# Hybrid decoder step: normalized x of a tile made in the token part, x loaded once per tile, index rings of four tiles

## The chip, the cores and the metric

One core of a Trainium2 chip runs the whole program. The metric is the device time of one execution in microseconds, the median of several. Engines are TensorE (PE), VectorE (DVE), ScalarE (ACT), GpSimd (POOL) and SyncE (SP, which only issues DMAs here); they run their own instruction streams and meet at semaphores.

## What is computed

One layer of a decoder for 1024 prompt tokens and 32 sample tokens (1056 in all, D = 1024). What matters here is its last part, PEER: each token picks 16 experts in each of 8 heads, 128 experts in all, and each expert is one row u and one row v of 1024 floats.

```python
x = x + merged
x = x + peer(rmsnorm(x, g_ffn), w_query, sub_keys, expert_u, expert_v)
...
u = expert_u[eid]
act = jax.nn.gelu(jnp.einsum('cd,ced->ce', xc, u))
return jnp.einsum('ce,ced->cd', g * act, expert_v[eid])
```

`rmsnorm(x, g)` is x times the reciprocal root of the mean square of its row, times g. The outputs end with a final RMSNorm with g_final.

## The kernel before

Tokens are cut into nine tiles: eight of 128 and one of 32. The program has two blocks. The **early** block makes the input projection, attention and merge of tiles 0 to 3. The **late** block runs the token part from its start to its end, and beside it, on the other engines' free time, the router (which experts a token takes) for tiles 0 to 3, then projection, attention, samples and merge of tiles 4 to 8, then the router for these.

The **merge** makes the residual x of a tile (`x2`), its mean square, the factor (`col(k, 11)`, L1676) and x times factor (`xn`, on ScalarE, L1614). TensorE turns that for the router (L1570), VectorE scales the turned form by g_ffn (L1688), and SyncE stores it as `x_turned` (L1503). For the token part VectorE also multiplies `xn` by a g_ffn row (`g_row`, L1681, loaded at L1430 once for each merge), and SyncE stores the residual as `x_res` (L1497) and the product as `x_norm` (L1499), both in HBM.

The **token part** (class `Tokens`) walks 1056 tokens, called steps n, in blocks of 16. For a step, GpSimd gathers 128 u rows by the indices in a column of `idx` (L1786, an indirect DMA of 512 KB into one of eight slots), VectorE makes the 128 dot products with the token's x (L1936), ScalarE takes the gelu of 16 tokens, VectorE makes the weights `w_sel` (L1953), GpSimd gathers the v rows (L1795, eight slots, by fours) and TensorE sums them (L1862). A u gather waits for the dot of eight steps before; a group of v gathers waits for the sums of two groups before. x gets to all partitions by a product with a selector on TensorE (`repeat_x`, L1834), one for 32 tokens, from `xn_tile`, which SyncE loads from `x_norm` once a tile (L1801, at step 97 of the tile before, when TensorE has repeated that tile's last part). When a tile is done, VectorE adds the residual (`resid`, loaded at L1801 after the tile before has been stored, L1818), and after a root on ScalarE it scales the rows by g_final (L1960 to L1976).

All of this is woven by hand: `Pace` says how many token steps every engine has done at each step of the stage beside it, so the order on each engine is fixed in the program, and each engine works through its own order.

Of the kernel before, what the change touches and what calls it, by code (L numbers as in the profile page):

```python
# [29 lines left out]
P = 128  # L30
# [1381 lines left out]
class OutWeights:  # L1412


    def __init__(self, s, a, take):
        self.a = a
        self.rnn, self.att, self.g_row = take("w_rnn", [P, CC, D]), take("w_att", [P, CC, D]), take("g_row", [P, D])
        self.landed = [s.sem(x) for x in ("w_rnn_landed", "w_att_landed", "g_row_landed")]
        self.scaled = [s.sem(x) for x in ("rnn_scaled", "att_scaled")]
# [15 lines left out]
def merge(nc, a, c, far, ctx, door, stage, tiles, yaT, take, banks, pace_of, here=None, weights=None, after_first=None):  # L1435
# [5 lines left out]
    for k in range(NT + LAG_N):  # L1441
# [12 lines left out]
    w_rnn, w_att, g_row = held.rnn, held.att, held.g_row  # L1454
    x_in, x2 = take("x_in2", [P, 2, D]), take("x2", [P, 2, D])
    xn, xf = take("xn2", [P, D]), take("xf", [P, 2, D])
    sq, xt = take("sq", [P, 2 * CC, P]), take("xt_out", [P, KC, P])
# [9 lines left out]
    xf_ready, xt_ready, xt_stored, nothing_ready = (  # L1467
        s.sem(x) for x in ("xf_ready", "xt_ready", "xt_stored", "nothing_ready"))
    xf_stored = [s.sem(f"xf_stored{i}") for i in range(2)]
# [8 lines left out]
    def sp_part(sp):  # L1478
# [15 lines left out]
        def store(k):  # L1494
# [3 lines left out]
            sp.wait_ge(xf_ready, k + 1)  # L1498
            sp.dma_start(far.x_norm[lo:lo + rows, :], xf[0:rows, k % 2, :]).then_inc(xf_stored[k % 2], 16)  # L1499
# [38 lines left out]
        for par in range(2):  # L1538
            sp.wait_ge(x2_stored[par], 16 * len(tiles[par::2]))
            sp.wait_ge(xf_stored[par], 16 * len(tiles[par::2]))  # L1540
# [49 lines left out]
    def act_part(act):  # L1590
# [9 lines left out]
        def second(k, x):  # L1600
            rows = rows_of_tile(k)
            whole = x2[0:rows, k % 2, :]
            if x == 0:
                act.wait_ge(x2_ready, 2 * (k + 1))
                if k:
                    act.wait_ge(xf_ready, k)
# [5 lines left out]
            if x == 2:  # L1612
                act.wait_ge(rb_ready, k + 1)
                nc.scalar.activation(xn[0:rows, :], whole, ACT.Copy, scale=col(k, 11)).then_inc(xn_ready, 1)  # L1614
# [25 lines left out]
    def dve_part(dve):  # L1640
# [28 lines left out]
        def second(k, x):  # L1669
# [34 lines left out]
        dve.wait_ge(held.landed[2], 16)  # L1704
# [26 lines left out]
V_SLOTS = 8  # L1731
TOPK = 16
# [11 lines left out]
class Tokens:  # L1744


    def __init__(self, nc, c, ctx, a, far, kept):
# [3 lines left out]
        self.idx, self.gate = sb("idx", [P, NTOK], I32), sb("gate_r", [P, NTOK])  # L1751
        self.u_rows, self.v_rows = sb("u_rows", [P, U_SLOTS, D]), sb("v_rows", [P, V_SLOTS, D])
        self.xn, self.sums = sb("xn_tile", [P, D]), sb("sums", [P, D])
        self.resid, self.y_out, self.gfin = sb("resid", [P, D]), sb("y_out", [P, D]), sb("gfin", [P, D])
# [6 lines left out]
        self.xn_landed, self.resid_landed, self.gfin_landed, self.out_landed = (  # L1761
            sem(x) for x in ("xn_landed", "resid_landed", "gfin_landed", "out_landed"))
# [13 lines left out]

    def pool_to(self, pool, upto):
        nc, a = self.nc, self.a
        for b, t in self.span("pool", upto):
            if b + 1 < NB:  # L1780
# [3 lines left out]
                if n >= U_SLOTS:  # L1784
# [3 lines left out]
                    bass.IndirectOffsetOnAxis(ap=self.idx[:, n:n + 1], axis=0)).then_inc(self.u_landed[n % U_SLOTS], 16)  # L1788
            if b >= 0 and t % GROUPS == GROUPS - 1:
# [4 lines left out]
                for n in range(first, first + GROUPS):  # L1794
                    nc.gpsimd.indirect_dma_start(  # L1795
                        self.v_rows[:, n % V_SLOTS, :], None, a["expert_v"][0],
                        bass.IndirectOffsetOnAxis(ap=self.idx[:, n:n + 1], axis=0)).then_inc(landed, 16)

    def load_tile(self, sp, whole, into, landed, tile):
        lo, rows = tile * P, NS if tile == PT else P  # L1800
        sp.dma_start(into[0:rows, :], whole[lo:lo + rows, :]).then_inc(landed, 16)  # L1801

    def sp_begin(self, sp):
        self.load_tile(sp, self.far.x_norm, self.xn, self.xn_landed, 0)
# [710 lines left out]
```

## Time and profile before

| | before |
|---|---|
| median of 3 runs | 3399.2 us (3398.39 to 3399.62) |
| profiled execution, its time | 3404.3 us |
| profiled execution, its span | 3402.1 us |
| VectorE busy | 2132.1 us (63%) |
| POOL busy | 2081.0 us (61%) |
| TensorE busy | 2042.7 us (60%) |
| DMA | 1251.30 MB, mean 368 GB/s |
| of these the gathers (software queue) | 1107.43 MB |

The profiled execution is one run under the profiler; its rows give durations, the median gives the time. Busy time counts instructions that compute or, on POOL, issue a gather. The token part begins at 381 us of the span. "Landing" is the time from a DMA's issue to its completion.

### The profile page before, as it was taken

The numbers are of one execution on the slowest core, as the hardware profiler recorded it, in microseconds if no ns is written. First come the engines' busy times: TensorE is split into PE (matmuls) and PEld (weight loads), VectorE is DVE, ScalarE is ACT, GpSimd is POOL, SyncE is SP. The second block draws the span as 40 slices with busy tenths as digits, with TensorE's granted clock in tenths as the row PEclk, the third lists the DMA queues.
The fourth block names the chain that finished last, engine by engine and source line by source line (L and its number), as shares of the span: only waits on it lengthen the run. The fifth ranks groups of instructions, "written<-read, shape, count | busy, mean of one in ns | idle before, by whom it ended". The sixth has DMA issues, their size and how long they took to land.

```text
span 3402.1 us, 28445 instructions
## 1 busy us (share of the span) xinstructions
PE 2042.7 (60%) x8758; PEld 793.8 (23%) x8758; DVE 2132.1 (63%) x5404; ACT 657.4 (19%) x1245; POOL 2081.0 (61%) x2144
## 2 busy tenths in 40 slices
PE   5989366574989577554775556445544654364343
PEld 2445232231554133211321212101110210021000
DVE  5253688986666577523564968756765676578542
ACT  2361121222223144200221112101110120011001
POOL 0200277776666666634565777777777777777773
PEclk9999687786999687766887778667866777687556
DMA  3342499999999999999999999999999999999995
GB/s 112 124 168 80 163 382 393 404 383 409 406 418 418 416 401 370 385 388 356 403 414 421 410 411 417 413 420 419 419 418 420 419 418 416 420 419 410 416 419 212
DMA packets 347553, 1251.30 MB, mean 368 GB/s; under 512 B 43258, under 2 KB 49402, under 8 KB 343052
## 3 DMA queue, kind: packets, MB, share of 16 engines
q0 software_dynamic: 304128, 1107.43, 81.2%
q1 hardware_dynamic: 43276, 142.07, 11.1%
q8 instruction: 70, 1.15, 0.1%
q14 instruction: 79, 0.65, 0.0%
HBM read 1219.39 MB, written 29.96 MB: 367 GB/s over the span
## 4 chain that ended last, share of the span: by engine, by line
POOL 27%; DVE 17%; DMA 16%; issue 13%; PE 13%; ACT 3%; SPq 1%; DVEq 0%; ACTq 0%; POOLq 0%
POOL v_rows L1795 15%; POOL u_rows L1786 12%; DMA u_rows<-expert_u,idx 8%; DVE u_rows L1936 7%; DMA v_rows<-expert_v,idx 6%; PE y_acc L1862 3%; PE pair L1561 2%; PE pair L598 1%; PE pair L618 1%; PE pair L2069 1%; PE pair L1008 1%; DMA arena<-w_out 1%; PE pair L1029 1%; DVE arena L2197 1%; DVE arena L2161 1%
## 5 line engine op out<-in xcount | busy, mean ns | idle before, releaser
L1936 DVE CUSTOM_DVE_ANT_0 u_rows<-u_rows,xb 128x1024 f32<-128x1024 f32 x1056 | 1271.3, 1214 | 643.9 <-DMA u_rows<-expert_u,idx 630.4
L1786 POOL DMA_INDIRECT u_rows<-expert_u,idx x1056 | 1029.1, 974 | 681.7 <-issue 258.1
L1862 PE MATMUL y_acc<-v_rows,w_sel 128*32 128x512 f32 x4224 | 791.6, 883 | 926.2 <-DMA v_rows<-expert_v,idx 869.3
L1795 POOL DMA_INDIRECT v_rows<-expert_v,idx x1056 | 1020.9, 967 | 481.6 <-issue 310.3
L1862 PEld LDWEIGHTS y_acc<-v_rows,w_sel 128*32 128x32 f32 x4224 | 145.4, 139 | 1435.1 <-DMA v_rows<-expert_v,idx 813.5
L2069 PE MATMUL pair<-arena 128*128 128x512 f32 x576 | 290.5, 639 | 0.0
L1894 ACT ACTIVATE acts<-dots 128x16 f32<-128x16 f32 x66 | 14.3, 216 | 794.2 <-DVE dots L1936 794.0
L598 PE MATMUL pair<-arena 128*128 128x272 f32 (+1 forms) x576 | 155.1, 428 | 2.2 <-DVEq L769 1.8
L2069 PEld LDWEIGHTS pair<-arena 128*128 128x128 f32 x576 | 108.8, 204 | 175.8 <-issue 175.8
L2097 PE MATMUL pair<-arena,selx 128*128 128x64 f32 x264 | 54.4, 371 | 132.5 <-DVE arena L2219 100.0
L598 PEld LDWEIGHTS pair<-arena 128*128 128x128 f32 x576 | 111.3, 196 | 54.0 <-issue 32.2
L598 PE MATMUL bank<-arena 128*128 128x512 f32 x192 | 86.3, 609 | 0.8 <-DVEq L769 0.8
L1936 DVE DVE_READ_ACCUMULATOR2_ANT dots<- 128x1 f32 x1056 | 86.7, 82 | 0.0
L2097 PEld LDWEIGHTS pair<-arena,selx 128*128 128x128 f32 x264 | 48.8, 276 | 161.4 <-DVE arena L2219 128.1
L1016 PE MATMUL pair<-ident,arena 128*128 128x128 f32 x225 | 44.3, 331 | 59.3 <-ACT arena L1074 43.3
L1907 ACT ACTIVATE y_out<-xb 32x1024 f32<-32x1024 f32 x33 | 33.5, 1016 | 234.7 <-PE xb L1872 234.7
L1114 DVE CUSTOM_DVE_ANT_0 arena<-pair,arena 128x512 f32<-128x512 f32 (+3 forms) x64 | 38.6, 618 | 63.4 <-PE pair L1008 63.4
L1834 PE MATMUL xb<-xn_tile,selx 128*128 128x512 f32 (+1 forms) x132 | 76.1, 705 | 1.5 <-DMA xn_tile<-x_norm 1.5
L1561 PE MATMUL pair<-arena 128*128 128x512 f32 (+1 forms) x160 | 74.4, 620 | 1.5 <-DVE arena L1688 1.4
L1872 PE MATMUL xb<-sums,rep 128*32 128x512 f32 x132 | 73.7, 687 | 0.8 <-ACT sums L1899 0.8
L2119 ACT ACTIVATE gate_r<-pair 32x32 f32<-32x32 f32 (+1 forms) x144 | 26.8, 186 | 234.2 <-PE pair L2097 233.0
L1899 ACT ACTIVATE sums<-y_acc 128x512 f32<-128x512 f32 x66 | 35.8, 594 | 187.8 <-PE y_acc L1862 187.7
(294 smaller groups left out, 2413.1 us busy)
## 6 DMA issues: line engine op xcount, KB each, us to landing
u_rows<-expert_u,idx POOLq DMA_INDIRECT x1056, 10.0
v_rows<-expert_v,idx POOLq DMA_INDIRECT x1056
arena<-w_in_tiles SPq DMA_DIRECT2D x32, 512.0 KB, 6.3
arena<-w_query_by_group SPq DMA_DIRECT2D x8, 2048.0 KB, 19.6
arena<-cache_kT SPq DMA_DIRECT2D x8, 1792.0 KB, 16.6
arena<-cache_v_near SPq DMA_DIRECT2D x8, 1024.0 KB, 10.3
arena<-x_prompt SPq DMA_DIRECT2D x12, 512.0 KB, 6.9
arena<-cache_v_old SPq DMA_DIRECT2D x8, 768.0 KB, 12.4
```

The source lines that it names most:

```text
L598: last = nc.tensor.matmul(ring.bank(n)[:, 0:hi - lo], w[:, use % 3, k * P:(k + 1) * P], xnT[:, k, lo:hi], start=(k == 0), stop=(k == KC - 1))
L1016: last = nc.tensor.transpose(ring.bank(n)[:, b:b + P], held(d, h)[:, lo + b:lo + b + P], c.ident[:])
L1114: nc.vector.tensor_tensor_reduce(out=logits[:, h, lo:hi], in0=ring.bank(n)[:, 0:hi - lo], in1=bias[:, edge + lo:edge + hi], scale=1.0, sca ...
L1561: last = nc.tensor.matmul(ring.bank(n)[0:rows, :], y_of(k, g, j), w_of(g)[:, j, half * HALF:(half + 1) * HALF], start=(j == 0), stop=(j == ...
L1786: nc.gpsimd.indirect_dma_start(self.u_rows[:, n % U_SLOTS, :], None, a["expert_u"][0], bass.IndirectOffsetOnAxis(ap=self.idx[:, n:n + 1], ...
L1795: nc.gpsimd.indirect_dma_start(self.v_rows[:, n % V_SLOTS, :], None, a["expert_v"][0], bass.IndirectOffsetOnAxis(ap=self.idx[:, n:n + 1], ...
L1834: last = self.nc.tensor.matmul(self.xb[:, k % 2, half:half + HALF], self.c.selx[0:rows, block, :], self.xn[0:rows, half:half + HALF], star ...
L1862: last = nc.tensor.matmul(self.acc[g * BAND:(g + 1) * BAND, half:half + HALF], self.w_sel[:, b % 2, n, :], self.v_rows[:, (TB * b + n) % V ...
L1872: last = self.nc.tensor.matmul(self.xb[block * BAND:(block + 1) * BAND, k % 2, half:half + HALF], self.c.rep[:], self.sums[:, half:half + ...
L1936: nc.vector.tensor_tensor_reduce(out=self.u_rows[:, n % U_SLOTS, :], in0=self.u_rows[:, n % U_SLOTS, :], in1=self.xb[:, n // BAND % 2, :], ...
L2069: last = self.nc.tensor.matmul(self.qp, self.xt[:, part, :], self.w[:, g * KC + part, :], start=(part == 0), stop=(part == KC - 1))
L2097: last = self.nc.tensor.matmul(self.wide[:, block], self.selx[:, block, :], self.found[:, :, ranks], start=True, stop=True)
```

## The change

The merge keeps, for each tile, only the row factors in a small tile `factor` (128 x 9) that stays in SBUF. The store of `x_norm`, the product that makes it, `g_row` and its two loads go. The token part loads the residual x of a tile once, into one of two halves of `x_tile`, at step 65 of the tile before, after the add of the tile before that; the same rows serve the add at the end. A g_ffn row (`gffn`) is loaded once at the start of the token part. VectorE makes `xn_tile` from x, factor and g_ffn in one operation (`normal`), ahead of the first dot of all and then ahead of the dot of step 100 of each tile. `idx` and `gate` hold four tiles in place of nine, and the ScalarE copies into them wait, from tile 4 on, for the sums of the tile that stood there.

```diff
-        self.rnn, self.att, self.g_row = take("w_rnn", [P, CC, D]), take("w_att", [P, CC, D]), take("g_row", [P, D])
+        self.rnn, self.att = take("w_rnn", [P, CC, D]), take("w_att", [P, CC, D])
...
-        if i == 0:
-            sp.dma_start(self.g_row, self.a["g_ffn"].to_broadcast((P, D))).then_inc(self.landed[2], 16)
...
+    factor = lambda k: c.factor[0:rows_of_tile(k), tiles[k]:tiles[k] + 1]
...
-            sp.wait_ge(xf_ready, k + 1)
-            sp.dma_start(far.x_norm[lo:lo + rows, :], xf[0:rows, k % 2, :]).then_inc(xf_stored[k % 2], 16)
...
-                nc.vector.reciprocal(col(k, 11), col(k, 10)).then_inc(rb_ready, 1)
-            if x == 2:
-                dve.wait_ge(xn_ready, k + 1)
-                if k >= 2:
-                    dve.wait_ge(xf_stored[k % 2], 16 * (k // 2))
-                nc.vector.tensor_tensor(xf[0:rows, k % 2, :], xn[0:rows, :], g_row[0:rows, :], ALU.mult).then_inc(xf_ready, 1)
+                nc.vector.reciprocal(factor(k), col(k, 10)).then_inc(rb_ready, 1)
...
-        self.idx, self.gate = sb("idx", [P, NTOK], I32), sb("gate_r", [P, NTOK])
+        self.idx, self.gate = sb("idx", [P, HELD * P], I32), sb("gate_r", [P, HELD * P])
...
     def sp_begin(self, sp):
-        self.load_tile(sp, self.far.x_norm, self.xn, self.xn_landed, 0)
+        self.load_tile(sp, 0)
+        sp.dma_start(self.gffn[:], self.a["g_ffn"].to_broadcast((P, D))).then_inc(self.gffn_landed, 16)
         sp.dma_start(self.gfin[:], self.a["g_final"].unsqueeze(0).to_broadcast((P, D))).then_inc(self.gfin_landed, 16)
-        self.load_tile(sp, self.far.x_res, self.resid, self.resid_landed, 0)
...
-            if block == 3 and (b + 1) % BB == 0 and t == 1 and b + 1 < NB:
-                sp.wait_ge(self.xb_ready, 4 * (tile + 1))
-                self.load_tile(sp, self.far.x_norm, self.xn, self.xn_landed, tile + 1)
+            if block == 2 and (b + 1) % BB == 0 and t == 1 and b + 1 < NB and tile < PT:
+                if tile:
+                    sp.wait_ge(self.added, tile)
+                self.load_tile(sp, tile + 1)
...
-                self.load_tile(sp, self.far.x_res, self.resid, self.resid_landed, tile + 1)
...
+                if n == 0:
+                    self.normal(dve, 0)
+                if n % P == P - BAND + 4 and n // P < PT:
+                    self.normal(dve, n // P + 1)
...
+    def normal(self, dve, tile):
+        rows = NS if tile == PT else P
+        dve.wait_ge(self.x_landed, 16 * (tile + 1))
+        if tile:
+            dve.wait_ge(self.xb_ready, P // BAND * tile)
+        else:
+            dve.wait_ge(self.gffn_landed, 16)
+        self.nc.vector.scalar_tensor_tensor(out=self.xn[0:rows, :], in0=self.x_res[0:rows, tile % 2, :],
+                                            scalar=self.c.factor[0:rows, tile:tile + 1], in1=self.gffn[0:rows, :],
+                                            op0=ALU.mult, op1=ALU.mult).then_inc(self.xn_ready, 1)
...
         blocks = 1 if r == PT else 4
+        if r >= HELD and g == 0:
+            act.wait_ge(self.tok.v_free, P * (r - HELD + 1))
```

Three places show how the order moves. First VectorE, where the early block ends and the token part begins; `factor`, `x_tile` and `gffn` are the new tiles, and the two rows L1936 (L1934 in the changed kernel) are one dot. Before:

```order
L2215 SCALAR_TENSOR_TENSOR arena<-arena 128x32
L2217 RECIPROCAL arena<-arena 128x2
L1936 ISA u_rows,dots<-u_rows,xb 128x1024
L1936 ISA dots 128x1
L2219 TENSOR_TENSOR arena<-arena 128x32
L2148 MAX arena<-arena 128x8 x4
```

and now:

```order
L2225 SCALAR_TENSOR_TENSOR arena<-arena 128x32
L2227 RECIPROCAL arena<-arena 128x2
L1961 SCALAR_TENSOR_TENSOR xn_tile<-x_tile,factor,gffn 128x1024
L1934 ISA u_rows,dots<-u_rows,xb 128x1024
L1934 ISA dots 128x1
L2229 TENSOR_TENSOR arena<-arena 128x32
```

One product of 128 x 1024 stands ahead of the first dot.

Second SyncE in the late merge, the stores of its last two tiles (tile 7 and the 32-row tile); `arena` is the merge's own space. Before:

```order
L1497 DMA x_res<-arena 128x1024
L1499 DMA x_norm<-arena 128x1024
L1503 DMA x_turned<-arena 128x1024
L1497 DMA x_res<-arena 32x1024
L1499 DMA x_norm<-arena 32x1024
L1503 DMA x_turned<-arena 1024x1x32
```

and now:

```order
L1495 DMA x_res<-arena 128x1024
L1499 DMA x_turned<-arena 128x1024
L1795 DMA x_tile<-x_res 128x1024
L1495 DMA x_res<-arena 32x1024
L1499 DMA x_turned<-arena 1024x1x32
```

The store of x_norm of each tile is gone (five in all in this merge), and a load of x into `x_tile` (tile 4) has come in between.

Third SyncE in a tile of the last stage, one period and a little more. Before:

```order
L1801 DMA xn_tile<-x_norm 128x1024
L2026 DMA arena<-x_turned 128x1024
L1818 DMA out_y_prompt<-y_out 128x1024
L1801 DMA resid<-x_res 128x1024
L2026 DMA arena<-x_turned 128x1024
L1801 DMA xn_tile<-x_norm 128x1024
```

and now:

```order
L2034 DMA arena<-x_turned 128x1024
L1813 DMA out_y_prompt<-y_out 128x1024
L2034 DMA arena<-x_turned 128x1024
L1795 DMA x_tile<-x_res 128x1024
L1813 DMA out_y_prompt<-y_out 128x1024
```

Of two loads a tile for the token part (`xn_tile` and `resid`) one is left, and it stands behind the load of the next turned tile, not behind the store of y.

## Rows read from the trace of the kernel before

**Rows 1.** Windows by stage: busy us of each engine, PEclk, DMA share, GB/s.

```profile
430.00:800.00 370.00, 240.85 (x1016) 99.03 (x1016) 338.40 (x1055) 77.81 (x193) 267.58 (x274) 0.80 1.00 393
800.00:1200.00 400.00, 301.45 (x1305) 155.84 (x1306) 242.67 (x498) 107.33 (x164) 262.45 (x269) 0.84 1.02 414
1200.00:1410.00 210.00, 153.42 (x957) 73.88 (x957) 149.89 (x361) 91.35 (x139) 142.66 (x146) 0.83 0.98 382
1410.00:1650.00 240.00, 110.82 (x658) 32.87 (x662) 73.33 (x152) 26.50 (x38) 96.16 (x102) 0.64 1.01 384
1650.00:1880.00 230.00, 165.01 (x652) 63.88 (x648) 135.19 (x277) 37.49 (x62) 141.28 (x146) 0.85 1.02 413
1900.00:3330.00 1430.00, 714.73 (x2964) 197.40 (x2964) 955.57 (x2336) 171.31 (x376) 1083.03 (x1121) 0.72 1.02 417
...
1480.00:1490.00 10.00, 5.28 (x33) 2.40 (x25) 5.08 (x13) 3.35 (x4) 2.50 (x3) 0.50 1.02 431
```

**Rows 2.** L1786, landings in windows 800:1200, 1410:1650, 1650:1880, 1900:2000, 3250:3330.

```profile
DMA to landing us min/median/max: 5.1/14.0/18.0
...
DMA to landing us min/median/max: 6.8/22.5/46.7
...
DMA to landing us min/median/max: 8.4/12.1/35.1
...
DMA to landing us min/median/max: 5.8/5.9/8.3
...
DMA to landing us min/median/max: 11.1/11.3/11.6
```

**Rows 3.** Timeline, last stage: gathers and VectorE products beside them.

```profile
2009.15 0.95 POOL L1786 DMA_INDIRECT u_rows<-expert_u,idx  x1 [0.30 <-issue]
2010.40 1.72 POOL L1786 DMA_INDIRECT u_rows<-expert_u,idx  x1 [0.30 <-issue]
...
3008.14 1.51 POOL L1786 DMA_INDIRECT u_rows<-expert_u,idx  x1 [0.30 <-issue]
...
2010.08 1.23 DVE L1960 TENSOR_TENSOR y_out<-y_out,resid 128x1024 f32<-128x1024 f32 x1 [1.35 <-ACT y_out L1907]
...
3007.55 1.28 DVE L1976 SCALAR_TENSOR_TENSOR y_out<-y_out,y_stat,gfin 128x1024 f32<-128x1024 f32 x1
```

**Rows 4.** Waits of POOL in 1900:3330: us in total, times, longest.

```profile
POOL u_rows L1786 <- DVE dots L1936: 29.6, 88, 1.4
```

**Rows 5.** The chain that ended last, 3300 to the end.

```profile
3333.16 12.90 DMA v_rows<-expert_v,idx
```

**Rows 6.** Timeline, end of the early merge: VectorE, ScalarE, SyncE.

```profile
355.39 0.16 DVE L1676 RECIPROCAL region<-region 128x1 f32<-128x1 f32 x1 [1.68 <-ACT region L1611]
358.82 1.22 DVE L1681 TENSOR_TENSOR region<-region 128x1024 f32<-128x1024 f32 x1 [0.59 <-ACT region L1614]
359.96 0.74 DVE L2171 MAX8 arena<-arena 128x8 f32<-128x256 f32 x2
...
369.31 0.68 DVE L1688 TENSOR_TENSOR region<-bank,g_ffn_T 128x512 f32<-128x512 f32 x1
...
368.15 0.60 ACT L2137 ACTIVATE arena<-pair 128x512 f32<-128x512 f32 x1 [1.31 <-PE pair L2086]
...
370.08 0.32 SPq L1503 DMA_DIRECT2D x_turned<-region  x1
```

**Rows 7.** Timeline, start of the token part, and a DMA issue row.

```profile
384.68 3.78 PE L1834 MATMUL xb<-xn_tile,selx 128*128 128x512 f32 x4 [1.50 <-DMA xn_tile<-x_norm]
...
390.77 1.22 DVE L1936 CUSTOM_DVE_ANT_0 u_rows<-u_rows,xb 128x1024 f32<-128x1024 f32 x1 [9.41 <-DMA u_rows<-expert_u,idx]
...
gfin<-g_final SPq DMA_DIRECT2D x1, 512.0 KB, 5.2
```

**Rows 8.** Timeline around the late merge's weights: SyncE and VectorE.

```profile
1598.55 6.30 SPq L1430 DMA_DIRECT2D arena<-g_ffn  x1
...
1642.15 2.74 DVE L1702 TENSOR_SCALAR arena<-arena,par 128x1024 f32<-128x1024 f32 x4 [20.61 <-DMA arena<-w_out]
```

More of the change, by code:

```diff
@@ L1416, in __init__ @@
         self.a = a
[L1417 to L1418 removed]
+        self.rnn, self.att = take("w_rnn", [P, CC, D]), take("w_att", [P, CC, D])
+        self.landed = [s.sem(x) for x in ("w_rnn_landed", "w_att_landed")]
         self.scaled = [s.sem(x) for x in ("rnn_scaled", "att_scaled")]
@@ L1453, in merge @@
     held = weights or OutWeights(s, a, take)
-    w_rnn, w_att, g_row = held.rnn, held.att, held.g_row
+    w_rnn, w_att = held.rnn, held.att
     x_in, x2 = take("x_in2", [P, 2, D]), take("x2", [P, 2, D])
-    xn, xf = take("xn2", [P, D]), take("xf", [P, 2, D])
-    sq, xt = take("sq", [P, 2 * CC, P]), take("xt_out", [P, KC, P])
+    xn = take("xn2", [P, D])
+    xt, sq = take("xt_out", [P, KC, P]), take("sq", [P, 2 * CC, P])
     yr = None if here else take("y_rnn", [P, 3, CC, P])
@@ L1466, in merge @@
         s.sem(x) for x in ("sqb_done", "msb_ready", "rtb_done", "rb_ready", "xn_ready"))
-    xf_ready, xt_ready, xt_stored, nothing_ready = (
-        s.sem(x) for x in ("xf_ready", "xt_ready", "xt_stored", "nothing_ready"))
-    xf_stored = [s.sem(f"xf_stored{i}") for i in range(2)]
+    xt_ready, xt_stored, nothing_ready = (
+        s.sem(x) for x in ("xt_ready", "xt_stored", "nothing_ready"))
     yr_of = lambda k: here.y[:, :, k * P:(k + 1) * P] if here else yr[:, k % 3, :, 0:rows_of_tile(k)]
@@ L1613, in second @@
                 act.wait_ge(rb_ready, k + 1)
-                nc.scalar.activation(xn[0:rows, :], whole, ACT.Copy, scale=col(k, 11)).then_inc(xn_ready, 1)
+                nc.scalar.activation(xn[0:rows, :], whole, ACT.Copy, scale=factor(k)).then_inc(xn_ready, 1)
         pace.act(act, -1)
@@ L1731 @@
 V_SLOTS = 8
+HELD = 4
 TOPK = 16
@@ L1775, in span, with column @@
         return [(x // TB - 1, x % TB) for x in steps]
+    def column(self, held, n, width=1):
+        at = n % (HELD * P)
+        return held[:, at:at + width]
     def pool_to(self, pool, upto):
@@ L1796, in pool_to, with load_tile @@
                         self.v_rows[:, n % V_SLOTS, :], None, a["expert_v"][0],
-                        bass.IndirectOffsetOnAxis(ap=self.idx[:, n:n + 1], axis=0)).then_inc(landed, 16)
-    def load_tile(self, sp, whole, into, landed, tile):
+                        bass.IndirectOffsetOnAxis(ap=self.column(self.idx, n), axis=0)).then_inc(landed, 16)
+    def load_tile(self, sp, tile):
         lo, rows = tile * P, NS if tile == PT else P
-        sp.dma_start(into[0:rows, :], whole[lo:lo + rows, :]).then_inc(landed, 16)
+        sp.dma_start(self.x_res[0:rows, tile % 2, :], self.far.x_res[lo:lo + rows, :]).then_inc(self.x_landed, 16)
     def sp_begin(self, sp):
-        self.load_tile(sp, self.far.x_norm, self.xn, self.xn_landed, 0)
+        self.load_tile(sp, 0)
+        sp.dma_start(self.gffn[:], self.a["g_ffn"].to_broadcast((P, D))).then_inc(self.gffn_landed, 16)
         sp.dma_start(self.gfin[:], self.a["g_final"].unsqueeze(0).to_broadcast((P, D))).then_inc(self.gfin_landed, 16)
-        self.load_tile(sp, self.far.x_res, self.resid, self.resid_landed, 0)
     def sp_to(self, sp, upto):
@@ L1828, in repeat_x @@
         rows = NS if tile == PT else P
-        pe.wait_ge(self.xn_landed, 16 * (tile + 1))
+        pe.wait_ge(self.xn_ready, tile + 1)
         if k >= 2:
@@ L1949, in dve_to @@
                 dve.wait_ge(self.gelu_done, ub + 1)
-                nc.vector.tensor_tensor(self.share[:], self.acts[:], self.gate[:, TB * ub:TB * (ub + 1)],
+                nc.vector.tensor_tensor(self.share[:], self.acts[:], self.column(self.gate, TB * ub, TB),
                                         ALU.mult).then_inc(self.share_ready, 1)
@@ L1958, in add @@
         dve.wait_ge(self.y_kept, min(P // BAND * (tile + 1), NTOK // BAND))
-        dve.wait_ge(self.resid_landed, 16 * (tile + 1))
-        self.nc.vector.tensor_tensor(self.y_out[0:rows, :], self.y_out[0:rows, :], self.resid[0:rows, :],
+        self.nc.vector.tensor_tensor(self.y_out[0:rows, :], self.y_out[0:rows, :], self.x_res[0:rows, tile % 2, :],
                                      ALU.add).then_inc(self.added, 1)
@@ L2113, in act_spread @@
         blocks = 1 if r == PT else 4
+        if r >= HELD and g == 0:
+            act.wait_ge(self.tok.v_free, P * (r - HELD + 1))
         for x, held in enumerate((self.tok.gate, self.tok.idx)):
-            here = held[:, P * r:P * r + BAND * blocks].rearrange("p (c i) -> p c i", i=BAND)
+            here = self.tok.column(held, P * r, BAND * blocks).rearrange("p (c i) -> p c i", i=BAND)
             for k in range(4):
@@ L2292, in __init__ @@
         self.x_res = dram("x_res", (NTOK, D))
-        self.x_norm = dram("x_norm", (NTOK, D))
         self.x_turned = dram("x_turned", (PT + 1, P, KC, P))
@@ L2323, in program @@
         c.selx, c.rep = s.sb("selx", [P, 4, P]), s.sb("rep", [P, BAND])
+        c.factor = s.sb("factor", [P, PT + 1])
         c.par, c.coef = s.sb("par", [P, CC, N_ROWS]), s.sb("coef", [P, 2, CC])
@@ L2350, in program @@
             merging = merge(nc, a, c, far, held, Doorway(left, 2), "merge_early", early, yaT,
-                            Arena(region, 2 * CC * D + D + 2 * CC * WAVE * P).take, banks, along, here, weights,
+                            Arena(region, 2 * CC * D + 2 * CC * WAVE * P).take, banks, along, here, weights,
                             lambda sp: router.load_tokens(sp, 0))
```

14 lines of the change are left out of this document (6 added, 8 removed).

## The prediction, on record before the changed kernel ran

> **What bounds the kernel now.** I read the windows by stage first [rows 1]. From 430 us on, the mean share of the DMA engines is 0.98 to 1.02 in every stage, so the 16 engines always have something to move. That doesn't yet say that bytes set the time, so I looked at who is waited for: how long a gather of u rows takes to land, and what GpSimd (POOL), which issues the gathers, waits for.
>
> The landing time tells the queue in front of the DMA engines [rows 2]. Just after 1900 us it is 5.9 us: that is a gather with next to no queue. In 800 to 1200 it is 14.0 us, in 1410 to 1650 22.5, in 1650 to 1880 12.1: there a queue stands, slots come back late, POOL issues fewer gathers, and bytes are time. In 1900 to 3330 it creeps up from 5.9 to 11.3 us.
>
> The long last stage (1900 to 3330, 1430 us) is paced by POOL itself. Two gathers follow each other every 1.25 us (2009.15, 2010.40) [rows 3], of which 0.95 is the instruction and 0.30 the gap. 1121 gathers [rows 1] x 1.25 = 1401 us; POOL's busy time is 1083.0, which is 18 above 1121 x 0.95, from gathers that took longer; together 1419 of the 1430 us. Its real waits there are nearly nothing: 88 waits for dots of 0.34 us each, of which 0.30 is the usual gap [rows 4]. So here fewer bytes don't make the pace faster. They only keep the queue from growing, which is paid at the end: the last v gather issued in pace (3333.16) takes 12.9 us to land and the end of the program hangs on it [rows 5].
>
> In 430 to 800 VectorE is 338.4 of 370 us busy [rows 1]: it sets the pace with the router's work. In 1200 to 1410 no queue stands (DMA at 382 GB/s) and VectorE, TensorE and POOL alternate.
>
> **The change part by part.** A tile of 512 KB is 0.524 MB, 1.27 us at 413 GB/s [rows 1]; one gather moves as much.
>
> (a) Early merge. Four products L1681 and four stores of x_norm go. Around 254 to 335 us TensorE is the bound and they are hidden. The last one isn't: VectorE has its factor at 355.39, then sits in order before L1681, which waits for the scaled x until 358.82 and takes 1.22; the router work behind it then runs to the last L1688 at 369.31, and SyncE's last store at 370.08 follows at once [rows 6]. Without it that work starts some 4 us earlier, but the next L1688 needs TensorE's transposes (which need the same scaled x), and ScalarE's last copy ends at 368.75. I take -2.7 us for the store; bounds 0 and -4.4 (the whole stretch from 355.55 to 359.96).
>
> (b) Start of the token part. Before, x_norm lands and TensorE repeats it at 384.68 for 3.78 us, ready 2.2 us before the first gather is used at 390.77 [rows 7]. Now the g_ffn row goes out in the place of g_final (5.2 us to landing; issued at some 381.4, so 386.6), then the product on VectorE (1.28, by L1976, the same operation and shape [rows 3]), then 3.78 on TensorE: 391.7, and the first dot moves to 391.8. +1.0; bounds 0 and +2.5.
>
> (c) 430 to 800. One product (for tile 1) on the busy VectorE: +1.3. The x_norm load that goes is replaced by the residual load that now comes here. Bounds 0 and +1.3.
>
> (d) 800 to 1200, bytes bound. Two tile loads fewer (two residual loads and one x_norm load before, one x load now): -1.05 MB at 414 GB/s = -2.5; bounds 0 and -2.5. Its product lies in waits for u rows.
>
> (e) 1200 to 1410. No queue, bytes free. The product for tile 3: half of 1.28, +0.6; bounds 0 and +1.3.
>
> (f) 1410 to 1650. The second load of the g_ffn row goes. SyncE spent 6.30 us issuing it, ahead of the eight w_out pieces, and VectorE stood 20.6 us until they had landed at 1642.15 [rows 8], with POOL waiting behind its dots. But the queue is full, so the last piece comes by bytes: 0.52 MB, -1.3. Bounds 0 and -6.3 (the whole issue time).
>
> (g) 1650 to 1880, bytes bound. Five x_norm stores (2.23 MB), a residual load and an x_norm load go, one x load comes (SyncE's rows of the late merge in the section on the change): -2.75 MB at 413 GB/s = -6.7; bounds -3 (if half lies beside the stage's own chain of TensorE and VectorE) and -6.7. The five L1681 products there are in VectorE's waits, worth nothing.
>
> (h) 1900 to 3330. Four products, one a tile, at the hundredth dot. VectorE has room (955.6 of 1430 us). But an operation of VectorE with two inputs in SBUF makes the gather beside it longer: beside L1960 (2010.08) the gather took 1.72, beside L1976 (3007.55) 1.51, against 0.95 [rows 3]. All four L1976 of the stage did so, and L1960 in three of five. I take 0.55 each: +2.2, straight on POOL's pace; bounds 0 and +3.8 (0.95 each). The Trainium skill (SBUF — State Buffer, Who interferes with whom) says that VectorE with two SBUF inputs contends with reads of GpSimd and not with its writes, and infers that descriptor generation needs only the write side; that would make this term 0. The rows contradict the inference for these indexed gathers, and the rows decide.
>
> (i) The end. After 1900 us 2.1 MB less are moved (four residual loads and four x_norm loads before, four x loads now): 5.0 us of queue, and (h) gives the engines 2.2 us more to catch up. So the 11.3 us of landing fall to the floor of 5.9: -5.4, paid once, at the gather of 3333.16. Bounds 0 and -7 (12.9 to 5.9).
>
> The ring of four tiles for idx and gate costs no instruction. ScalarE's new wait asks for the v rows of a tile four back, while the router is one tile ahead of the tokens: never late. The load now waits for the add of the tile before, done some 40 steps earlier; SyncE is held less than by the old wait for xb.
>
> Sum: -2.7 +1.0 +1.3 -2.5 +0.6 -1.3 -6.7 +2.2 -5.4 = -13.5 us. The profiled execution took 3404.3 us, 0.15% above the median of 3399.2; the difference is taken from the median: 3385.7.
>
> **Rivals.**
> - All bytes pay at once: the 6.5 MB that leave after 430 us at 416 GB/s = 15.6, with (a), and 5.0 of SyncE's issue time in (f), less 5.1 for the products in (b), (c), (e) and (h): -18.2, 3381.0. For it: the share of 1.0 throughout. Against it: a floor of 5.9 in parts of the last stage.
> - The queue at the end isn't the DMA engines' own limit, and doesn't shrink with the bytes: without (i) -8.1, 3391.1. For it: in 1900 to 3330 the mean is 417 GB/s while a window with many cache loads has 431 [rows 1], so there may be room. The Trainium skill (DMA: Bandwidth & Descriptors, Where 436 GB/s comes from) has a ceiling of 436 GB/s; by it 419 GB/s of gathers would leave 4% free and no queue would build. The trace has one that grows from 5.9 to 11.3 us, which speaks against.
> - The stages' own chains set the time in 800 to 1880, and bytes only stood beside them: (d), (f), (g) are 0: -3.0, 3396.2. For it: in the late merge TensorE and VectorE are busy 165 and 135 of 230 us and wait for each other. Against it: landing 12 to 22 us, and POOL issues 146 gathers in 230 us there [rows 1], one per 1.58 us, where it could do 1.25.
> - Slower: the products stand ahead of the dots. Each holds the next dot back by 1.28, the slot comes back that much later, and POOL, which has eight u slots, stops. Nine times 1.28 = 11.5, with 3.8 of longer gathers, (a) and (i), and no byte that pays: +7.2, 3406.4. It decides from the point where a slot's round (landing, dot, reissue) exceeds 8 x 2.5 = 20 us; there landing is 11.3 to 12.9 [rows 2, 5], so some 5 us are to spare. Against it, then, in the last stage at least.
>
> **How the numbers follow.** Chances: the forecast 0.42, all bytes 0.20, no gain at the end 0.16, chains 0.16, slower 0.06. 0.2% is 6.8 us, about what can be told from no change. Faster by more: the forecast and all bytes nearly whole (0.60) and most of the third (0.14): 0.74. Same: 0.20. Slower: 0.06. The range goes from beyond "all bytes" with (a) and (f) at their bounds, 3377, to "chains", 3397.
>
> **What would show it.** (a) the last SyncE store of the early merge about 3 us earlier; (b) first dot about 1 us later after the barrier; (d), (g) stages 800 to 1200 and 1650 to 1880 shorter by 2.5 and 6.7 at the same GB/s; (h) four gathers beside the new product at 1.3 to 1.8, and the time for the 1121 gathers 2 us longer, not shorter; (i) landing near 6 us at 3300, and the last v gather in pace landing in 6 to 8 us. I am wrong if the landing at the end stays above 10, if the last stage gets shorter by the bytes, or if POOL's waits for dots grow.

## The result, and the profile after

The changed kernel is slower: 3439.8 us median (3436.3 to 3442.2, 4 runs) against 3399.4 us for the kernel before (3398.4 to 3399.7, 4 runs), taken beside it. The ratio is 1.0116, 95% interval 1.0104 to 1.0129. The prediction was 3385.7 us, with 0.06 on slower. The profiled execution took 3436.26 us (span 3434.4).

The windows by stage of the changed kernel, with the columns of [rows 1]:

```profile
430.00:800.00 370.00, 244.28 (x1016) 99.77 (x1016) 337.04 (x1049) 75.89 (x192) 267.12 (x272) 0.78 1.00 391
800.00:1200.00 400.00, 295.69 (x1288) 152.81 (x1280) 236.78 (x485) 101.15 (x155) 259.83 (x265) 0.85 1.02 405
1200.00:1410.00 210.00, 152.31 (x915) 72.04 (x917) 148.87 (x361) 93.28 (x141) 141.89 (x144) 0.81 0.99 379
1410.00:1650.00 240.00, 111.28 (x721) 33.66 (x713) 75.72 (x153) 29.06 (x42) 99.80 (x106) 0.67 1.02 378
1650.00:1880.00 230.00, 160.09 (x642) 61.72 (x643) 132.10 (x271) 38.31 (x63) 138.28 (x144) 0.82 1.03 411
1900.00:3330.00 1430.00, 707.29 (x2920) 200.09 (x2924) 946.59 (x2319) 166.80 (x370) 1065.65 (x1099) 0.69 1.02 407
```

Against [rows 1], the DMA share is the same 1.02 in the long stages, but the engines move less in it: 405 instead of 414 GB/s in 800 to 1200, and 407 instead of 417 after 1900, 2.4% less. In the last stage POOL issues 1099 gathers instead of 1121. In 430 to 800, where VectorE sets the pace, the rate is nearly as before (391, 393).

How long a u gather takes to land in the changed kernel, in 1900 to 2000 and in 3250 to 3330 (compare [rows 2]):

```profile
DMA to landing us min/median/max: 5.9/6.7/7.8
...
DMA to landing us min/median/max: 12.7/12.8/13.0
```

What POOL waited for in 1900 to 3330, apart from issuing (compare [rows 4]; us in total, times, longest). The first two rows are the changed kernel's, the third is the kernel before:

```profile
POOL v_rows L1789 <- PE y_acc L1856: 36.2, 47, 2.0
POOL u_rows L1780 <- DVE dots L1934: 22.1, 66, 1.1
...
POOL v_rows L1795 <- PE y_acc L1862: 2.8, 3, 1.1
```

The landing at the end is 12.8 us, not 6: the queue is longer than before. POOL, which waited 2.8 us for v slots before, waits 36.2 us for them, 47 times. POOL no longer paces the stage alone: slots come back late because the DMA engines move less. The chain that ended last in the changed kernel shows the same at its end; its v gather in pace takes 12.66 us where [rows 5] has 12.90:

```profile
3367.56 12.66 DMA v_rows<-expert_v,idx
3380.26 3.69 PE y_acc L1856 x16
...
3387.95 5.76 DMA v_rows<-expert_v,idx
```

The bytes did leave: the page has 1242.12 MB for the changed kernel and 1251.30 MB for the one before, with the same 1107.43 MB of gathers. So the change did what it says, and the bytes that stay became dearer.

The start went as the prediction had it. SyncE's last store of the early merge and the first rows of the token part (compare [rows 6, 7]):

```profile
366.65 0.32 SPq L1499 DMA_DIRECT2D x_turned<-region  x1
377.37 0.33 SPq L1795 DMA_DIRECT2D x_tile<-x_res  x1
...
383.62 1.28 DVE L1961 SCALAR_TENSOR_TENSOR xn_tile<-x_tile,factor,gffn 128x1024 f32<-128x1024 f32 x1 [5.93 <-DMA gffn<-g_ffn]
...
388.78 1.22 DVE L1934 CUSTOM_DVE_ANT_0 u_rows<-u_rows,xb 128x1024 f32<-128x1024 f32 x1 [3.87 <-PE xb L1828]
```

The store stands at 366.65 instead of 370.08 and the first dot at 388.78 instead of 390.77.

**Where the time appears.** A gather has the same number in every version, so its start is a clock for the program. The durations below are the differences of POOL's start times of the u gathers 0, 128, 256, 384, 512 and 1054 in the timelines of the profiled executions, and from there to the end of the span (us):

| kernel | start of 0 | to 128 | to 256 | to 384 | to 512 | to 1054 | to the end | span |
|---|---|---|---|---|---|---|---|---|
| before | 385.1 | 338.2 | 367.5 | 390.2 | 466.3 | 1379.6 | 75.2 | 3402.1 |
| changed | 381.4 | 342.5 | 372.3 | 394.4 | 462.7 | 1407.3 | 73.7 | 3434.4 |
| e1 | 383.6 | 340.3 | 367.1 | 390.7 | 465.1 | 1381.7 | 69.0 | 3397.4 |
| e2 | 385.9 | 338.3 | 373.7 | 395.3 | 469.8 | 1415.1 | 77.0 | 3455.1 |
| e3 | 381.4 | 340.0 | 371.5 | 393.8 | 463.2 | 1407.3 | 75.0 | 3432.1 |
| e4 | 383.4 | 342.4 | 367.9 | 390.5 | 455.1 | 1388.7 | 68.2 | 3396.1 |
| e6 | 381.2 | 339.8 | 368.5 | 389.7 | 464.4 | 1377.3 | 73.8 | 3394.7 |
| e7 | 386.9 | 338.3 | 367.1 | 391.9 | 458.8 | 1376.6 | 73.2 | 3392.9 |
| e8 | 383.6 | 339.7 | 364.6 | 390.6 | 453.8 | 1375.9 | 72.3 | 3380.4 |
| e9 | 381.2 | 342.3 | 368.9 | 390.4 | 459.7 | 1378.2 | 72.5 | 3393.2 |
| e10 | 382.7 | 340.1 | 371.0 | 394.6 | 461.1 | 1409.1 | 74.5 | 3433.1 |

Each row is one execution, and executions of one version spread by some 11 us (e1 from 3388.3 to 3399.4, e4 from 3387.0 to 3398.0), so a difference of two or three us in one column says little. The e numbers are the experiments below.

The spans differ by 32.3 us (the profiled execution of the kernel before was a long one). Of this, 27.7 us lie between gather 512 and 1054, and 4 to 5 us in each of the three columns to 128, 256 and 384; the column to 512, which holds the late merge, is shorter. In the last stage the loss comes evenly: u gathers 768 to 1024 take 667.4 us instead of 653.1, 2.2% more. That is a price per gather, not an event. The column to 128 doesn't belong to it: e4 and e9 have the same 342 us there without the loss, and e2 has the loss with 338.3.

### The profile page after: what moved, and what is told of

Its sections match the earlier page's. It is cut to its first block, busy times and chain, and to the rows that moved or that the text cites. A ratio compares the mean times of both kernels' runs of the same rounds, so it can differ in the third digit from the quotient of the medians.

```text
span 3434.4 us, 28416 instructions
## 1 busy us (share of the span) xinstructions
PE 2036.5 (59%) x8758; PEld 791.9 (23%) x8758; DVE 2133.1 (62%) x5404; ACT 657.2 (19%) x1245; POOL 2088.2 (61%) x2144
## 2 busy tenths in 40 slices
DMA packets 345009, 1242.12 MB, mean 362 GB/s; under 512 B 42954, under 2 KB 49098, under 8 KB 340508
## 3 DMA queue, kind: packets, MB, share of 16 engines
q0 software_dynamic: 304128, 1107.43, 81.9%
## 4 chain that ended last, share of the span: by engine, by line
DMA 26%; POOL 17%; PE 16%; DVE 16%; issue 10%; ACT 2%; another core or an unknown queue 0%; DVEq 0%; ACTq 0%; SPq 0%; POOLq 0%
DMA v_rows<-expert_v,idx 13%; DMA u_rows<-expert_u,idx 11%; POOL v_rows L1789 11%; DVE u_rows L1934 7%; POOL u_rows L1780 6%; PE y_acc L1856 6%; PE pair L1556 2%; PE pair L598 2%; PE pair L2077 1%; PE pair L618 1%; DMA arena<-cache_kT 1%; PE pair L1008 1%; PE pair L1029 1%; DMA arena<-cache_v_old 1%; DVE arena L2207 1%
## 5 line engine op out<-in xcount | busy, mean ns | idle before, releaser
L1934 DVE CUSTOM_DVE_ANT_0 u_rows<-u_rows,xb 128x1024 f32<-128x1024 f32 x1056 | 1273.3, 1216 | 670.5 <-DMA u_rows<-expert_u,idx 646.8
L1789 POOL DMA_INDIRECT v_rows<-expert_v,idx x1056 | 1033.9, 979 | 511.5 <-issue 293.3
L1934 DVE DVE_READ_ACCUMULATOR2_ANT dots<- 128x1 f32 x1056 | 87.5, 83 | 0.0
L1866 PE MATMUL xb<-sums,rep 128*32 128x512 f32 x132 | 73.7, 687 | 0.8 <-ACT sums L1893 0.8
```

Source lines behind the costliest of these rows:

```text
L1789: nc.gpsimd.indirect_dma_start(self.v_rows[:, n % V_SLOTS, :], None, a["expert_v"][0], bass.IndirectOffsetOnAxis(ap=self.column(self.idx, ...
L1866: last = self.nc.tensor.matmul(self.xb[block * BAND:(block + 1) * BAND, k % 2, half:half + HALF], self.c.rep[:], self.sums[:, half:half + ...
L1934: nc.vector.tensor_tensor_reduce(out=self.u_rows[:, n % U_SLOTS, :], in0=self.u_rows[:, n % U_SLOTS, :], in1=self.xb[:, n // BAND % 2, :], ...
```

## The experiments

**The theories.** What costs per byte and wasn't in the working: where the bytes go. The change adds `factor` (36 bytes a partition, which takes 64) ahead of the arena in SBUF, and everything allocated behind it moves. The addresses per partition in the two compiled programs, with the remainder by 256:

```
            before            changed
arena       20736   (0)       20800   (64)
u_rows     134912   (0)      130624   (64)
v_rows     167680   (0)      163392   (64)
```

Theory P (placement): each of a gather's rows of 4096 bytes now starts between two multiples of 256, and the DMA engines take some 2.4% longer for it. Rival R1: x_norm is gone from HBM, so the tensors behind it have other addresses there. Rival R2: the change's own work (products, waits, the load's place) slows the gathers.

**e1, factor padded.** The changed kernel with everything that stands behind `factor` moved back to multiples of 256. `region` belongs to the early block and starts where `idx` starts later, so its length moves nothing:

```diff
-REGION = 25700
+REGION = 25600
...
-        c.factor = s.sb("factor", [P, PT + 1])
+        c.factor = s.sb("factor", [P, 64])
```

> The changed kernel with its new tile factor made 256 bytes a partition instead of 36 (and the arena's region shortened by 100 words), so that everything allocated behind it in SBUF, arena, u_rows and v_rows among it, starts again on a multiple of 256 bytes a partition as in the kernel before; no instruction is added, taken away or moved. Placement theory (the gathers and loads land 64 bytes off and the DMA engines take some 2.4% longer for them): about 3386 us, landing after 1900 us near 6 us and 416 to 420 GB/s. Rival, the change's own work or its HBM addresses: 3440 us, as the changed kernel, 405 to 410 GB/s in the last stage.

3396.8 us median (12 runs) against 3400.2 (23 runs), ratio 0.9984 (0.9975 to 0.9993). A tile of 64 floats in the place of 9 takes the whole loss of 40 us away, with the same work and the same tensors in HBM, so R1 and R2 fall as its cause. Of the gain of 13.5 us that was predicted, 3 us are there by the medians and 5 by the ratio.

**e2, before shifted.** The other way round, on the kernel before:

```diff
+        pad = s.sb("pad", [P, 16])
         arena = s.sb("arena", [P, ARENA])
```

> The kernel before with an unused tile of 64 bytes a partition allocated ahead of the arena, so that arena, u_rows and v_rows start 64 bytes behind a multiple of 256; nothing else is changed. Placement theory: slower by what the placement costs, 3399 + 54 = 3453 us, with some 407 GB/s in the last stage. Rivals (the change's own products, loads and waits, or HBM addresses): 3399 us, 417 GB/s.

3456.2 us (4 runs), ratio 1.0162 (1.0148 to 1.0177): 56 us for an unused tile of 64 bytes. The last stage reads:

```profile
1900.00:3330.00 1430.00, 709.95 (x2923) 197.68 (x2921) 943.70 (x2336) 166.79 (x370) 1057.97 (x1093) 0.70 1.02 407
```

The same 407 GB/s as in the changed kernel, with none of its edits. The loss is larger here than in the changed kernel, 56 us against 40; the section on the prediction comes back to this.

**e3, x_norm kept.** The changed kernel with the tensor still declared in HBM:

```diff
         self.x_res = dram("x_res", (NTOK, D))
+        self.x_norm = dram("x_norm", (NTOK, D))
```

> The changed kernel with x_norm still declared in HBM though nothing writes or reads it, so that every tensor in HBM has the address that it had in the kernel before. HBM address theory: 3386 to 3399 us. SBUF placement theory and the theory that the change's own work is to blame: 3440 us both.

3442.3 us (4 runs), ratio 1.0127 (1.0112 to 1.0141), and 407 GB/s after 1900. The HBM addresses have no part in it.

**e4, rows aligned.** Only the gathers' targets and the tiles behind them on multiples of 256; arena, region, idx and gate stay 64 bytes off:

```diff
+        self.pad = sb("pad", [P, 48])
         self.u_rows, self.v_rows = sb("u_rows", [P, U_SLOTS, D]), sb("v_rows", [P, V_SLOTS, D])
```

> The changed kernel with 192 unused bytes a partition ahead of u_rows: u_rows, v_rows and what is allocated behind them start on multiples of 256 bytes again, while arena, region, idx and gate stay 64 bytes off. Placement theory with the gathers' targets as the cause: 3386 to 3395 us. If the placement of arena and region (merge loads, stores) were the cause, or no placement at all: 3440 us.

3395.0 us (10 runs), ratio 0.9978 (0.9968 to 0.9988). The targets of the gathers are what counts: the tiles behind them, which move along, take part in under 1% of the bytes, and the placement of arena and region, which take and give most of the other 11%, shows nothing here. The landing at 3250 to 3330 is now near the floor, as the prediction's term (i) had it:

```profile
DMA to landing us min/median/max: 6.1/6.2/6.8
```

**e5, the gathers alone.** Eight slots, indexes made by an iota, nothing beside them, one execution; the target moved by an offset in floats (`LOADS` has pairs of target and source):

```python
GATHERS = [0, 16, 0, 32, 8, 1, 48]
LOADS = [(0, 0), (16, 0), (32, 0), (0, 16), (16, 16)]
...
        def slot(off, i):
            return rows[:, off + i * D:off + (i + 1) * D]
```

> None of the reference's computation, its outputs are left unwritten: 120 gathers of 128 rows of 4 KB from expert_u for each of seven places of the target in SBUF (0, 64, 0, 128, 32, 4 and 192 bytes behind a multiple of 256 a partition), with eight slots and nothing else beside them, then 120 plain loads of the same size on the queues of SyncE and ScalarE for each of five pairs (target and source 0 or 64 bytes off, target 128 off). Theory that pieces are cut at 256 bytes of the target: 0 keeps POOL's pace of 1.25 us a gather (419 GB/s); 4, 32, 64, 128 and 192 all drop alike, to some 1.29 us (407 GB/s). Theory of a 64-byte or 128-byte unit: 64 or 128 would run as 0 does. Theory that no placement matters when nothing else runs: all seven alike at 1.25 us.

Windows of the steady part of each phase, in the order of the two lists (columns: window, length, POOL busy, PEclk, DMA share, GB/s):

```profile
30.00:130.00 100.00, 75.28 (x82) 1.00 1.03 420
190.00:290.00 100.00, 74.24 (x80) 1.00 1.03 410
350.00:450.00 100.00, 75.28 (x82) 1.00 1.03 420
510.00:610.00 100.00, 75.40 (x81) 1.00 1.03 410
670.00:770.00 100.00, 74.89 (x80) 1.00 1.03 410
830.00:930.00 100.00, 74.91 (x81) 1.00 1.03 409
1000.00:1080.00 80.00, 60.35 (x65) 1.00 1.03 410
1140.00:1240.00 100.00, 0.00 (x0) 1.00 1.03 420
1280.00:1380.00 100.00, 0.00 (x0) 1.00 1.03 410
1430.00:1530.00 100.00, 0.00 (x0) 1.00 1.03 410
1580.00:1680.00 100.00, 0.00 (x0) 1.00 1.03 419
1740.00:1840.00 100.00, 0.00 (x0) 1.00 1.03 410
```

420 GB/s with the target on a multiple of 256, 409 to 410 when it is 4, 32, 64, 128 or 192 bytes off; plain loads the same (420 and 410). Two things about the size of the effect: it does not grow with the offset, and the source may lie 64 bytes off for 419. The plain loads keep eight in flight, and each takes 10.0 us to land (10.2 with the target off), eight times the 1.25 us that 512 KB take at 420 GB/s. So 420 and 410 are ceilings here.

The gathers reach them too. Alone, POOL issues one in 1.24 us, which asks for 422 GB/s. Their landing, aligned (30 to 130) and then 64 bytes off (190 to 290):

```profile
DMA to landing us min/median/max: 6.4/6.7/6.9
...
DMA to landing us min/median/max: 7.1/8.7/10.0
```

In the kernel a gather takes 1.25 us when nothing lengthens it (419 GB/s), and with the longer ones and the other traffic the last stage moves 413 to 417 GB/s on the mean with aligned targets (413 in e4, 415 in e1, 417 in the kernel before). That lies between the two ceilings. This is why the change was felt: before, the ceiling stood just above what the stage asks for, after it below.

The Trainium skill (DMA: Bandwidth & Descriptors, How a descriptor splits into AXI transactions) has reads cut at multiples of 256 bytes, with a further transaction for one that starts between two. The loads with a source 64 bytes off show next to nothing of it (419 against 420 GB/s); the side on which this case finds the price, the written one, the page doesn't speak of. That 17 pieces in the place of 16 are the cause would fit the unit of 256, but no run counted pieces.

**e6 and e9, half of the gathers.** dots (64 bytes) between u_rows and v_rows of e4, so that v_rows is off; and the mirror, the changed kernel's u_rows off and v_rows put right:

```diff
+        self.u_rows = sb("u_rows", [P, U_SLOTS, D])
+        self.dots = sb("dots", [P, TB])
+        self.v_rows = sb("v_rows", [P, V_SLOTS, D])
```

```diff
+        self.u_rows = sb("u_rows", [P, U_SLOTS, D])
+        self.pad = sb("pad", [P, 48])
+        self.v_rows = sb("v_rows", [P, V_SLOTS, D])
```

> As the changed kernel with its gather targets on multiples of 256 (3395 us), but dots (64 bytes a partition) now stands between u_rows and v_rows, so that v_rows and the tiles behind it lie 64 bytes off while u_rows doesn't: half of the gathers land misaligned. If each misaligned gather costs its own share: 3395 + 23 = 3418 us. If the cost is only what exceeds POOL's pace of 1.25 us a gather (aligned ones have slack that the others can use): well under half, 3397 to 3405 us.

> The mirror of the run with v_rows off: in the changed kernel u_rows stays 64 bytes off, and 192 unused bytes stand behind it so that v_rows and the tiles after it start on multiples of 256. Theory of a ceiling (half of the gathers at 410 and half at 420 GB/s give 415, just under the 416 to 419 that POOL's pace and the other traffic ask for, so the queue grows and the pace holds): as there, 3396 us, with 11 us of landing at 3300. Rival, that only the u gathers' targets matter and the v gathers' don't: 3440 us.

e6: 3396.0 us (10 runs), ratio 0.9986 (0.9977 to 0.9996). e9: 3395.3 us (10 runs), ratio 0.9978 (0.9960 to 0.9996). Either half alone costs nothing that can be told from e1 and e4, both together cost some 44 us. The window of the last stage in e6, and the landing of its u gathers in 3250 to 3330:

```profile
1900.00:3330.00 1430.00, 711.55 (x2968) 196.38 (x2972) 959.25 (x2336) 170.53 (x371) 1084.11 (x1121) 0.70 1.02 416
```

```profile
DMA to landing us min/median/max: 11.0/11.0/11.6
```

The same two views of e9:

```profile
1900.00:3330.00 1430.00, 716.97 (x2972) 198.04 (x2972) 959.96 (x2333) 169.65 (x367) 1084.22 (x1121) 0.70 1.02 415
```

```profile
DMA to landing us min/median/max: 8.8/9.7/10.4
```

Both windows have 1121 gathers, so POOL's pace is as before. This is the ceiling at work: half at 410 and half at 420 make 415 (an estimate from e5), the stage asks for about as much, so the queue grows (landing 11.0 and 9.7 instead of 6.2) but the eight slots of each kind take it up. Of the two theories for e6, "each pays its share" (3418) fell; the other, 3397 to 3405, was still a little too dear. For e9 the ceiling gave 3396 and a landing of 11 us, against 3395.3 and 9.7.

**e10, 128 bytes off.** e4 with a pad of 64 bytes instead of 192:

```diff
-        self.pad = sb("pad", [P, 48])
+        self.pad = sb("pad", [P, 16])
```

> The changed kernel with 64 unused bytes a partition ahead of u_rows, so that u_rows, v_rows and what is behind them lie 128 bytes off a multiple of 256 instead of 64. Theory that only multiples of 256 count, as the gathers alone showed (410 GB/s at 128 as at 64): 3440 us, as the changed kernel. If 128 is enough beside the kernel's other traffic: 3395 us.

3438.7 us (4 runs), ratio 1.0105 (1.0062 to 1.0148), 407 GB/s after 1900. As in e5, 128 is no better than 64.

**e7, the bytes alone.** With the placement put right the change is worth 5 to 8 us by the ratios (3 to 5 by the medians) and not 13.5, so its terms were priced one kind at a time. The kernel before with x_norm's late stores and its tile loads cut to one row each:

```diff
-            sp.dma_start(far.x_norm[lo:lo + rows, :], xf[0:rows, k % 2, :]).then_inc(xf_stored[k % 2], 16)
+            sp.dma_start(far.x_norm[lo:lo + (rows if tiles[k] < WAVE else 1), :], xf[0:(rows if tiles[k] < WAVE else 1), k % 2, :]).then_inc(xf_stored[k % 2], 16)
...
+        if into is self.xn and tile:
+            rows = 1
```

> The kernel before with the traffic of x_norm cut to one row a transfer: the late merge stores one row of each tile instead of 128 and the token part loads one row of each tile from the second on, so the normalized x of those tokens is that of the first tile; no instruction is added or taken away. This prices the bytes of the change alone: 2.0 MB of stores in 1650 to 1880, and 3.7 MB of loads, half of them after 1900 us. By the prediction's terms (bytes where a queue stands, and a shorter landing at the end): -13 us, 3387. If bytes only stood beside the stages' own chains and the landing at the end has other causes: -2 to 0, 3398.

3395.4 us (12 runs), ratio 0.9984 (0.9973 to 0.9994): -5.4 us, -2 to -9. The 13 us of the prediction's byte terms lie outside the interval. By the table, one execution each, the columns to 256 and 384 give nothing together (759.0 against 757.7), the late merge gives 7.5, the last two columns 5.0 (1449.8 against 1454.8). The queue at the end did not vanish; the first v gather of the final chain still took:

```profile
3325.95 10.57 DMA v_rows<-expert_v,idx
```

**e8, the products cut.** e4 with the new product on 8 of 1024 columns for the tiles from the second on:

```diff
+        w = 8 if tile else D
-        self.nc.vector.scalar_tensor_tensor(out=self.xn[0:rows, :], in0=self.x_res[0:rows, tile % 2, :],
+        self.nc.vector.scalar_tensor_tensor(out=self.xn[0:rows, 0:w], in0=self.x_res[0:rows, tile % 2, 0:w],
```

> The changed kernel with aligned gather targets (3395 us), in which the product that normalizes x works on 8 columns instead of 1024 for the tiles from the second on (so those tokens use mostly the first tile's normalized x); waits, loads and order stay. It prices the products: by the prediction's terms 1.3 in 430 to 800, 0.6 in 1200 to 1410 and 2.2 of longer gathers after 1900 us, so 4 us faster, 3391. If VectorE's order costs more (the product ahead of a dot holds the slots back): 9 to 11 us faster, 3385. If nothing hangs on them: 3395.

3388.7 us (12 runs, from 3382.0 to 3398.3), ratio 0.9974 (0.9963 to 0.9985), against 0.9978 for e4: 1.4 us by the ratios, 6.3 by the medians, whose intervals overlap. The predicted 4 us lie between. The 9 to 11 us that the products would cost if they held the slots back don't show, but where the price lies between 0 and 6 us can't be told from this run.

The products' effect on the gathers can be read directly. The first of the four in the last stage, in the timelines of e1 and of e8:

```profile
2206.30 1.28 DVE L1961 SCALAR_TENSOR_TENSOR xn_tile<-x_tile,factor,gffn 128x1024 f32<-128x1024 f32 x1
2206.85 1.55 POOL L1780 DMA_INDIRECT u_rows<-expert_u,idx  x1 [0.30 <-issue]
...
2190.46 0.22 DVE L1963 SCALAR_TENSOR_TENSOR xn_tile<-x_tile,factor,gffn 128x8 f32<-128x8 f32 x1
2189.68 0.94 POOL L1781 DMA_INDIRECT u_rows<-expert_u,idx  x1 [0.30 <-DVE dots L1935]
```

The gathers beside the four products took 1.55, 1.79, 1.46 and 1.26 us in e1 instead of 0.95: 2.3 us together, against 2.2 in term (h). In e4 it was 2.8 us. In e8, with the product cut to 8 columns, all four took 0.94, so it is the product that lengthens them. In the changed kernel itself the products met the gathers otherwise (1.13, 1.12, 1.14 and 1.01) and cost 0.6 us.

## Why the prediction was wrong

**The step that failed** is the one that took the rate of the DMA engines as given. Every byte term was priced "at 413 GB/s" or 414 from [rows 1], with the remark that stages 800 to 1200 and 1650 to 1880 would be shorter "at the same GB/s"; the new tile `factor` has no term in the sum, which puts it at nothing without a reason, and of the ring it says that it "costs no instruction". True of instructions, but a tile also has a place. Both edits move the targets of all 2112 gathers: the shorter rings by 4352 bytes, which is 17 times 256 and harmless, the factor by 64, which is not. The runs put 43 to 45 us in its place: 3439.8 against 3396.8 and 3395.0 for the same kernel with aligned targets (e1, e4), and 56 us on the kernel before (e2). An estimate from e5: 1107.43 MB of gathers take 64 us longer at 410 than at 420 GB/s; where POOL or VectorE paces, a part of it is hidden. The rivals had no such case, and the one that ended slower (products ahead of dots) is not what happened: e1 has the same products and is not slower. Of the signs that the prediction named for being wrong, the first came (a landing above 10 us at the end, 12.8); POOL's waits for dots, the sign of that rival, fell from 29.6 to 22.1 us.

**How little room there was.** The reading that POOL paces the last stage at 1.25 us was right and is what makes this case sharp: the stage moved 417 GB/s on the mean, 0.7% below the ceiling of 420. The prediction saw the queue grow from 5.9 to 11.3 us and wondered whether there was room up to 431 GB/s. e5 shows none above 420 for such rows. The 436 GB/s that it takes from the Trainium skill (DMA: Bandwidth & Descriptors, Where 436 GB/s comes from) no run here reached. A resource at 99% should have been asked what would make it 2% dearer, not only what relieves it.

**What the same bytes are worth on either side of the ceiling.** e2 and the changed kernel have the same placement (64 bytes off) and the same 407 GB/s, and the changed one is the faster by 16 us (3439.8 against 3456.2; ratios 1.0116 and 1.0162). The 6.5 MB that by the prediction's count leave after 430 us are 16 us at 407 GB/s, an estimate. So where the ceiling lies below what the stages ask for, the rival "all bytes pay" (18.2 us) fits, though no run took these bytes away by themselves with the targets off; with aligned targets the same change is worth 5 to 8 us.

**Its other steps**, read on the four versions in which the placement costs no time (e1, e4, e6, e9; table above, against the kernel before, one execution each, so within two or three us):

| step | predicted | measured, e1 / e4 / e6 / e9 |
|---|---|---|
| (a)+(b) start of gather 0 | -1.7 | -1.5 / -1.7 / -3.9 / -3.9 |
| (c) to 128 | +1.3 | +2.1 / +4.2 / +1.6 / +4.1 |
| (d)+(e) to 384 | -1.9 | +0.1 / +0.7 / +0.5 / +1.6 |
| (f)+(g) to 512 | -8.0 | -1.2 / -11.2 / -1.9 / -6.6 |
| (h)+(i) to the end | -3.2 | -4.1 / +2.1 / -3.7 / -4.1 |
| sum, by the spans | -13.5 | -4.7 / -6.0 / -7.4 / -8.9 |

- (a), (b): right within some 2 us; the start moved as told.
- (c): the column is 1.6 to 4.2 us longer, but that is not shown to be the product's price: e8, without the product of tile 1, has 1.5 there as well (339.7 against 338.2). By gather 128 the start's gain is gone in most versions; what takes it back stays open.
- (d): wrong. Landings of 14 us in 800 to 1200 were taken as bytes being time; 1.05 MB less gave nothing in four versions, nor did e7's part of it. The stage moves 414 GB/s where e5 has a ceiling of 420, so it seems that a queue stands there at times and bytes still are not what it waits for all along; with the ceiling at 410 the same two columns lost 9.0 us. The "chains" rival was right for this stage, in the sense that fewer bytes bring nothing; which engine holds it in their place was not tested.
- (f), (g): the mean of -5.2 is nearer to the 8.0 than to nothing, yet it spreads over 10 us between versions that differ in placement alone, and e4, which gains 11.2, gives 9.1 back in the column to 1054. From gather 384 to the end the four are 5.3, 9.1, 5.6 and 10.7 us shorter, against 11.2 in the prediction. e7 gives 7.5 for its bytes in one execution. What in the late merge decides between -1 and -11 was not settled.
- (h): right in mechanism and size for e1 and e4, as the rows above show; in the changed kernel the size was 0.6. The inference of the Trainium skill (SBUF — State Buffer, Who interferes with whom) that descriptor generation is free of VectorE's reads does not hold for these gathers, by the 1.26 to 1.99 us of e1 and e4 against the 0.94 of e8.
- (i): right where all targets are aligned. The landing fell to 6.2 us (e4), and the tail from 75.2 to 69.0 (e1) and 68.2 us (e4), -6.2 and -7.0 against -5.4. In e6 and e9, with a ceiling of 415, the queue stays (11.0 and 9.7 us) and the tail gains 1.4 and 2.7, but the pace is kept.

With aligned targets the change is 0.9984 (0.9975 to 0.9993, e1) and 0.9978 (0.9968 to 0.9988, e4), 5 to 8 us faster than the kernel before. The two can't be told apart, and the forecast of 13.5 was too large for both, by (c), (d) and the unsettled (f), (g). The range of 3377 to 3397 holds both medians, near its upper end; what it left out is the placement.

## What to carry to other kernels

An edit that adds, drops or resizes a tile moves every tile allocated behind it: compare the addresses of the DMA targets before and after, and keep the targets of the heavy streams on multiples of 256 bytes a partition (seen here for rows of 4 KB). Here, with the demand one or two per cent below the DMA ceiling, transfers 2.4% dearer cost 2.2% in the last stage, and half of that only a longer queue and no time, so look at how far the demand stands below the ceiling before pricing either direction. When a change costs a constant share per gather over a thousand gathers, look at what all of them share, not at the edited instructions.

## What the runs showed of the hardware that was not expected

- Rows of 4 KB from HBM into SBUF: 420 GB/s with the target on a multiple of 256 bytes a partition, 409 to 410 at 4, 32, 64, 128 and 192 bytes off, for indexed gathers and plain loads alike (e5, e10). The profile's DMA share is 1.02 to 1.03 in both, so it doesn't tell the two apart; GB/s does.
- A source that starts 64 bytes behind a row's start in HBM: 419 GB/s, next to free (e5).
- With half of the gathers off, in either half, 415 to 416 GB/s and no time lost (3396.0 and 3395.3 us, e6 and e9); with both off 407 GB/s and 3439.8 us.
- A VectorE product of 128 x 1024 with two inputs in SBUF makes the indexed gather beside it take 1.26 to 1.99 us in place of 0.94 (e1, e4 against e8).
